# RWKV time mix: outputs of chunks 0 and 1 stand together behind chunk 1's state, those of 2 and 3 behind the last solution; the solutions go into two tiles in turn

## What is computed

```python
def step(state, inp):
    r_t, w_t, k_t, v_t, kk_t, a_t = inp
    sa = jnp.einsum('bhij,bhj->bhi', state, -kk_t)
    state = (state * w_t[:, :, None, :]
             + sa[..., None] * (kk_t * a_t)[:, :, None, :]
             + v_t[..., None] * k_t[:, :, None, :])
    y_t = jnp.einsum('bhij,bhj->bhi', state, r_t)
    return state, y_t
```

## Time and profile before

| | |
|---|---|
| median of 3 runs | 1813.86 us (1811.67 to 1813.9) |
| the profiled execution, its own time | 1814.15 us |
| its span, first to last instruction | 1812.3 us |
| TensorE busy | 1755.4 us (97%) |
| VectorE busy | 846.5 us (47%) |
| ScalarE busy | 728.9 us (40%) |

### The profile page before, as it was taken

How to read it: one execution, slowest core, us unless ns; L and a number is a source line. 1 busy time by engine, 2 the same in 40 slices (tenths; PEclk the granted TensorE clock), 3 DMA queues, 4 the chain that set the end, 5 groups by cost and what they waited for, 6 DMA issues and landing times.

```text
span 1812.3 us, 22240 instructions
## 1 busy us (share of the span) xinstructions
PE 1755.4 (97%) x9406; PEld 1446.2 (80%) x9406; DVE 846.5 (47%) x1220; ACT 728.9 (40%) x1093; POOL 514.2 (28%) x115
## 2 busy tenths in 40 slices
PE   7999998999999999999999999999999999999997
PEld 6897777888877788878888888787778888888886
DVE  2015248898989963351123443608755411123343
ACT  5234364555556543252223222525662422222222
POOL 3432310000000002524444444333234354444442
PEclk9999998999999999999999999999999999999999
DMA  4431240001100133422222222221122222222221
GB/s 174 167 133 49 86 151 27 25 27 38 40 27 24 30 111 140 146 98 93 93 93 93 104 105 93 98 99 57 63 91 93 105 93 93 93 99 110 93 93 70
DMA packets 55158, 159.46 MB, mean 88 GB/s; under 512 B 3439, under 2 KB 33007, under 8 KB 40340
## 3 DMA queue, kind: packets, MB, share of 16 engines
q1 hardware_dynamic: 42620, 135.80, 21.4%
q10 hardware_dynamic: 12440, 22.24, 3.5%
HBM read 150.41 MB, written 9.19 MB: 88 GB/s over the span
## 4 chain that ended last, share of the span: by engine, by line
PE 83%; DVE 9%; ACT 4%; issue 2%; POOL 1%; DMA 1%; ACTq 0%; DVEq 0%
PE ps L616 24%; PE ps L618 23%; PE ps L617 23%; PE ps L1062 2%; POOL w_lo L607 1%; PE ps L1050 1%; ACT w_hi L1326 1%; PE ps L1140 1%; DVE x_res L2052 1%; PE ps L979 1%; DVE inverse L2356 1%; PE ps L1104 1%; DVE ht_lo L2035 1%; PE ps L1070 1%; PE ps L791 1%
## 5 line engine op out<-in xcount | busy, mean ns | idle before, releaser
L607 POOL TENSOR_TENSOR w_lo<-w_raw,w_hi 128x2048 fp32r<-128x2048 f32 x111 | 514.0, 4631 | 1268.0 <-ACT w_hi L1326 1268.0
L616 PE MATMUL ps<-ht_hi,w_hi 128*128 128x512 f32 (+1 forms) x1304 | 523.8, 402 | 14.5 <-DVE ht_lo L2035 4.7
L618 PE MATMUL ps<-ht_hi,w_lo 128*128 128x512 f32 (+1 forms) x1304 | 500.0, 383 | 0.0
L617 PE MATMUL ps<-ht_lo,w_hi 128*128 128x512 f32 (+1 forms) x1304 | 499.4, 383 | 0.0
L1326 ACT ACTIVATE w_hi<-w_raw 128x2048 fp32r<-128x2048 f32 x126 | 241.3, 1916 | 460.7 <-PE ps L618 408.9
L616 PEld LDWEIGHTS ps<-ht_hi,w_hi 128*128 128x128 f32 x1304 | 249.0, 191 | 75.6 <-issue 21.6
L618 PEld LDWEIGHTS ps<-ht_hi,w_lo 128*128 128x128 f32 x1304 | 248.7, 191 | 48.6
L617 PEld LDWEIGHTS ps<-ht_lo,w_hi 128*128 128x128 f32 x1304 | 249.6, 191 | 39.6 <-issue 1.7
L2572 DVE TENSOR_TENSOR hid_lo<-hidden,hid_hi 128x1024 fp32r<-128x1024 f32 x27 | 129.3, 4788 | 149.1 <-ACT hid_hi L1857 149.1
L616 PE MATMUL ps<-w_hi,hid_hi 128*128 128x512 f32 x432 | 168.3, 389 | 0.0
L618 PE MATMUL ps<-w_hi,hid_lo 128*128 128x512 f32 x432 | 168.1, 389 | 0.0
(11 more groups left out here) (326 smaller groups left out, 2372.2 us busy)
## 6 DMA issues: line engine op xcount, KB each, us to landing
w_raw<-in_wpack SPq DMA_DIRECT2D x114, 1024.0 KB, 4.8
w_raw<-in_wpack SPq DMA_DIRECT2D x24, 512.0 KB, 5.2
x_res<-in_x SPq DMA_DIRECT2D x4, 512.0 KB, 6.4
gate_back<-gate_dram ACTq DMA_DIRECT2D x2, 1024.0 KB, 7.1
gate<-gate_dram ACTq DMA_DIRECT2D x1, 2048.0 KB, 8.3
x_res<-in_x ACTq DMA_DIRECT2D x1, 2048.0 KB, 7.8
out_x<-y_tok ACTq DMA_DIRECT2D x4, 512.0 KB, 4.0
bias_skewed_dram<-bias_rows_dram ACTq DMA_DIRECT2D x1, 1792.0 KB, 10.8
```

The costliest lines, as they stand in the source:

```text
L607: nc.gpsimd.tensor_tensor(Wl[:, slot, :], raw[:, slot, :], f32(Wh[:, slot, :]), ALU.subtract).then_inc(lo_ready, 1)
L616: mm(dst, wh, ah, start=first, stop=False)
L617: mm(dst, wh, al, start=False, stop=False)
L618: return mm(dst, wl, ah, start=False, stop=last)
```

## The change

`chunk_out` is taken apart. The state of chunk t keeps its place (`chunk_state`). The outputs of chunk 0 are no longer issued behind its state but with those of chunk 1, behind chunk 1's state; those of chunk 2 go with those of chunk 3 (`chunk_outs`). In such a block of eight matmuls the order of a chunk is both heads by the values, then both heads by the solution. Since chunk t's solution is still needed when that of chunk t + 1 is written, `SA` becomes two tiles; the odd one lies in the last 128 columns of the tile `rwkv_out`. The start flags of bank 2 follow the new order.

```diff
-        SA = r("sa_sb", [P, P])
+        SA = [r("sa_sb_even", [P, P]), place("sa_sb_odd", [P, P], at=x_at + 4 * (PAIRS * T - P))[0]]
...
-                    mm(ps[:, 2, tok(t)], S[:], ra[:, t, 0, :], start=True, stop=False)
+                    mm(ps[:, 2, tok(t)], S[:], ra[:, t, 0, :], start=t < NT - 1, stop=False, skip_group_check=True)
...
+            def chunk_state(a, t):
+                w("sa_ready", NT, a, t + 1)
+                mm(ps[:, 3, 2 * P:3 * P], TB[:, t, :], SA[t % 2][:], start=True, stop=False)
+                last = mm(ps[:, 3, 2 * P:3 * P], TK[:, t, :], TV[:, t, :], start=False, stop=True)
+                inc(last, "s_full")
+
+            def chunk_outs(a, t0):
+
+                w("sa_ready", NT, a, t0 + 2)
+                for t in (t0, t0 + 1):
+                    for h in range(2):
+                        mm(ps[heads(h), 2, tok(t)], TV[:, t, heads(h)], GM[h][:, t, 0, :], start=False, stop=False,
+                           skip_group_check=True)
+                    for h in range(2):
+                        last = mm(ps[heads(h), 2, tok(t)], SA[t % 2][:, heads(h)], GM[h][:, t, 2, :], start=False, stop=t > t0,
+                                  skip_group_check=True)
+                if t0:
+                    inc(last, "y_full")
+
             def chunk_out(a, t):
-                w("sa_ready", NT, a, t + 1)
                 if t < NT - 1:
-                    mm(ps[:, 3, 2 * P:3 * P], TB[:, t, :], SA[:], start=True, stop=False)
-                    last = mm(ps[:, 3, 2 * P:3 * P], TK[:, t, :], TV[:, t, :], start=False, stop=True)
-                    inc(last, "s_full")
-                for h in range(2):
-                    mm(ps[heads(h), 2, tok(t)], TV[:, t, heads(h)], GM[h][:, t, 0, :], start=t == 0, stop=False)
-                    last = mm(ps[heads(h), 2, tok(t)], SA[:, heads(h)], GM[h][:, t, 2, :], start=False, stop=True)
-                if t == NT - 1:
-                    inc(last, "y_full")
+                    chunk_state(a, t)
+                if t % 2:
+                    chunk_outs(a, t - 1)
...
-                inc(actf(SA[:], ps[:, 3, P:2 * P], ACT.Copy), "sa_ready")
+                inc(actf(SA[t % 2][:], ps[:, 3, P:2 * P], ACT.Copy), "sa_ready")
```

## The result

The changed kernel takes 1818.52 us (median of 7 runs, 1815.49 to 1825.81) where the kernel before takes 1813.46 (7 runs, 1808.95 to 1815.81): a ratio of 1.0039, 95% interval 1.0022 to 1.0056. That is 5 us slower by the medians and 7 by the ratio, and 4 to 10 by its interval. The profiled execution took 1820.05 us. I had forecast 1815.0, no measurable change, and the measured median lies above my range.

A forecast was written before the change was run, and what follows sets the result against it. TensorE was taken to bound the recurrence, VectorE close behind. Pairs 0 to 4 +1.35, pair 5 +0.75, pair 6 +0.02 and pair 7 -1.02 gave +1.1 us on 1813.86: 1815.0 us, range 1811.5 to 1818.3.

The forecast's parts named there:

- What bounds the kernel: Recurrence: TensorE bounds it, VectorE close behind; line 1042 after chunk 0 waits for VectorE's line 2344, starting 0.05 to 0.06 us later.
- Chunk 0, "Gain 0": Pairs 0 to 6: the block ahead of line 1042 only covered a wait, so moving it gains 0; TensorE idles some 0.7 us.
- Chunk 1, +0.31: Pairs 0 to 6: the block grows by 0.44 us, a wait of 0.13 takes up part, +0.31 us each.
- The block of eight: Eight output matmuls issued together take about 0.59 + 0.44 = 1.03 us to the next line 616.
- Chunk 2, -0.48: Block removed ahead of line 1092: -0.48 us each in pairs 0 to 4, 0 in pair 5, -0.73 in pair 6.
- Chunk 3, +0.44: The block grows by 0.44 us and nothing takes it up, pairs 0 to 6; in pair 7 it is hidden, 0.
- The sum: All pairs: +1.35 for pairs 0 to 4, +0.75 pair 5, +0.02 pair 6, -1.02 pair 7, together +1.1 us.
- (A): Rival: TensorE's busy time decides, each of 16 moved blocks saves 0.29 us, -4.6 us, 1809.2 us; chance 0.09.
- (B): Rival: chunk 2's gain falls out because its state ends later, 3.7 us on top of +1.1, 1818.7 us; chance 0.11.
- the gain at chunk 0: 0 to 0.1: Bound at chunk 0: line 1042's first records may come closer behind the wait, -0.7 us on the sum.
- 0.29 us a block: Cost of going from matmuls of 128 columns to those of 64 and back, saved once per moved block by tiling-mode rule.

The follow-up runs named there:

- cover4: Changed kernel plus chunk 0's four output matmuls issued a second time in their old place, pairs 0 to 6; ratio 1.0003 to the kernel before.
- cover_wide: Changed kernel plus one full-form matmul (384 columns moving) ahead of line 1042, pairs 0 to 6; ratio 1.0015 to the kernel before.
- late_and_last: Against the kernel before: chunk 2's outputs go to chunk 3 in all pairs, chunk 0's to chunk 1 only in pair 7; ratio 1.0000.
- half_block: Against the kernel before: chunk 0's value products move to chunk 1, solution products of chunks 0 and 1 left out, pairs 0 to 6; ratio 1.0012.
- early_only: Against the kernel before: only chunk 0's outputs move to chunk 1, those of chunks 2 and 3 stay in place; ratio 1.0036.
- late_only: Against the kernel before: only chunk 2's outputs move to chunk 3, those of chunks 0 and 1 stay in place; ratio 1.0000.

## Why the prediction was wrong

**What bounds the kernel: right as far as it went.** Line 1042 starts 0.05 to 0.06 us behind VectorE's line in all seven pairs of the changed kernel as well.

**Chunk 0, "Gain 0": the step that failed.** I wrote "The cover that it gave is lost, and nothing else" and "TensorE stands idle for some 0.7 us more there", and put nothing on it. The idle time came out as written, 0.67 where 0.07 had been. Its price is not 0 but the granted clock: 1.23 to 1.60 us for each pair that is hit, four pairs in the profile, 6.0 us. `cover4` against the changed kernel shows that it is this idle time and not the order of the blocks. I had the earlier trace rows with a clock of 1.00 in front of me and used it as a constant. It had been measured with TensorE idle for 0.07 us at this place, and an edit that makes it 0.67 had to be priced with a loss of clock among its bounds: the stretch of half clock in pair 1, 371.4 to 374.8 us, is 3.4 us long and would cost half of that, 1.7, if TensorE never waited in it; 1.59 was measured.

**Chunk 1, +0.31: right,** +0.26 to +0.28 in the table for pairs 0 to 6 (and +0.18 in pair 7, where +0.26 was forecast). The block of eight takes what I said, 1.03 us from 433.09 to 434.12 in pair 2 of the changed kernel:

```profile
433.09 0.44 PE L1118 MATMUL ps<-gram,v_chunk 128*64 128x128 f32 x4
433.36 0.39 PE L1121 MATMUL ps<-gram,sa_sb_even 128*64 128x128 f32 x4
433.58 0.39 PE L1118 MATMUL ps<-gram,v_chunk 128*64 128x128 f32 x4
433.80 0.39 PE L1121 MATMUL ps<-gram,sa_sb_odd 128*64 128x128 f32 x4
434.12 0.50 PE L616 MATMUL ps<-ht_hi,w_hi 128*128 128x512 f32 x1
```

**Chunk 2, -0.48: right,** -0.50 to -0.53 in pairs 0 to 4, -0.04 in pair 5 (0 forecast), -0.85 in pair 6 (-0.73). What I left out is the same as at chunk 0: in pair 5 the moved block had filled a wait, which grows from 0.16 to 0.76 us. It cost nothing in the profile of the changed kernel, but half clock begins there in two other profiles (`cover_wide`, `late_and_last`). Pair 2 of the changed kernel: the state ends at 441.00 and line 1092 starts at 441.06.

```profile
440.65 0.35 DVE L2401 SCALAR_TENSOR_TENSOR state<-state,mid_decay,consts 128x128 f32<-128x128 f32 x1
...
441.06 0.49 PE L1092 MATMUL ps<-state,ra 128*128 128x128 f32 x2
```

**Chunk 3, +0.44: right but for one pair.** From the last column to the next pair's line 1042 it is +0.47 to +0.51 in pairs 0 to 4, but -0.01 in pair 5. There TensorE already waited 0.46 us for VectorE's line 2358 ahead of line 1050 before the change, which I had not looked up; the longer block fills that wait. The row of before:

```profile
597.40 0.64 PE L1050 MATMUL ps<-tinv,level 128*128 128x128 f32 x4 [0.46 <-DVE tinv L2358]
```

**The sum** without the clock is about +0.2 us, against my +1.1: about half of the difference is pair 5, 0.12 is chunk 2 of pair 6, the rest hundredths in each step. These terms were mis-sized; the mechanism held.

**The rivals.** (A) had the blocks gain at chunk 0, which they don't. (B) forecast the side and nearly the time, 1818.7, but by a wait at chunk 2 that never came; being near by its number is no merit. The case that happened was none of mine. The bound on "the gain at chunk 0: 0 to 0.1" was the narrowest of all and the wrong one: it had no loss in it.

The Trainium skill, page "TensorE: Matmul & The Clock Gate", Part 1, says that the clock gate follows how busy TensorE has been recently, and that activity releases the throttle. The trace agrees as far as it goes, in the windows at 0.50 above, most of which begin behind an idle TensorE; no run shows what makes the one at 310 us. In the prediction I weighed the page on tiling modes, which concerned 0.29 us a block, and not this one.

**What stays open:** which pairs are hit. With the same idle time it was four and three pairs in two profiles of the changed kernel, and two each in `half_block` and `early_only`. That windows begin behind this idle time and that none begins there with the cover is shown; when 0.67 us is followed by one is not. Nor is it shown what begins the window of pair 0 at 310 us, in two profiles, one of them with chunk 0 covered.

## What to carry to other kernels

Work on TensorE that only fills a wait can still be worth its place: ask of each moved instruction not only whether something waits for it, but how long the engine stands still without it. When an edit opens an idle gap of some tenths of a microsecond on a nearly always busy TensorE, put the half clock on the list of costs, at about 1.6 us a time here, and look at the granted clock by windows, not at the busy share, which is 100% in the slow windows. When one profile is compared with another, count the half clock outside of the changed stage too, and compare the mean clocks of the runs before calling a spread of a few microseconds noise.

## What the hardware showed that I had not expected

An idle gap of 0.67 us ahead of line 1042 (0.62 in pair 0, 1.00 in pair 6), with one of 0.37 us and mostly one of 0.12 to 0.22 close by, was followed by half clock in 4 and 3 of 7 places in two profiles of the same kernel. With at most 0.08 us in its place (0.35 to 0.42 in pair 6) it was in none of 7, in each of the profiles of the kernel before, `late_only`, `cover4`, `cover_wide` and `late_and_last`. The starts of successive matmuls of 512 columns go from 0.23 to 0.43 us apart then.

The two heads' output matmuls run side by side, whichever way they are written: before the change the order was values, solution, values, solution, but the trace has all four records of line 1114 ahead of those of line 1115, and a block of four took 0.59 us to the next line 616 in both orders (before, and `late_only` at chunk 1).
